# Retention: the next values are summed ahead of a unit's second rotation, and one of two barriers between the blocks is left out

## The reference, cut to what matters

```python
def rotary(t, pos):
    t1, t2 = t[..., :half], t[..., half:]
    return jnp.concatenate([t1 * cos - t2 * sin, t2 * cos + t1 * sin], -1)

def retention(q, k, v):                     # q and k rotated, blocks of 128 tokens
    scores = jnp.einsum('bnihd,bnjhd->bnhij', qc, kc) * dmask[None, None]
    inner = jnp.einsum('bnhij,bnjhe->bnihe', scores, vc)
    kv = jnp.einsum('bnjhd,hj,bnjhe->bnhde', kc, zeta, vc)
    def step(state, kv_n):
        return g_chunk[None, :, None, None] * state + kv_n, state
    _, prev = lax.scan(step, zeros, jnp.moveaxis(kv, 1, 0))
    cross = jnp.einsum('bnihd,hi,bnhde->bnihe', qc, xi, prev)
    return (inner + cross).reshape(b, lp, h, dv)
```

## Time and profile before

| what | us |
|---|---|
| median of 3 runs | 2862.14 (2860.37 to 2864.8) |
| the profiled execution | 2878.77 |
| its span, first to last instruction | 2876.9 |
| TensorE busy in the span | 2799.6 (97%) |
| VectorE busy | 1707.1 (59%) |
| GpSimd busy | 1347.0 (47%) |
| ScalarE busy | 621.4 (22%) |
| retention, first to last product (line 1053) | 151.9 to 624.1 |
| the granted TensorE clock, mean | 0.994 of full |

### The profile page before, as it was taken

How to read it: one execution, slowest core, us unless ns; L and a number is a source line. 1 busy time by engine, 2 the same in 40 slices (tenths; PEclk the granted TensorE clock), 3 DMA queues, 4 the chain that set the end, 5 groups by cost and what they waited for, 6 DMA issues and landing times.

```text
span 2876.9 us, 40988 instructions
## 1 busy us (share of the span) xinstructions
PE 2799.6 (97%) x14586; PEld 2066.1 (72%) x14586; DVE 1707.1 (59%) x4617; ACT 621.4 (22%) x1276; POOL 1347.0 (47%) x1140
## 2 busy tenths in 40 slices
PE   8999999999999999998999989999999999999997
PEld 4488888888876666664555767878878777787765
DVE  6655656657347777773777445677677772323226
ACT  2222222210025555551101101011111111111115
POOL 3533434547731111111455245677667665565535
PEclk9999999999999999999999999999999999999999
DMA  6500010111121113006444357899899989999986
GB/s 223 188 6 17 15 46 1 30 30 30 44 64 38 62 40 134 25 29 241 151 144 154 125 223 227 257 290 278 270 281 286 283 278 296 307 301 311 316 248 253
DMA packets 192573, 470.52 MB, mean 164 GB/s; under 512 B 27384, under 2 KB 108104, under 8 KB 166632
## 3 DMA queue, kind: packets, MB, share of 16 engines
q1 hardware_dynamic: 145424, 347.63, 33.8%
q0 software_dynamic: 44640, 111.84, 16.7%
q10 hardware_dynamic: 2304, 8.39, 0.7%
HBM read 349.64 MB, written 118.11 MB: 163 GB/s over the span
## 4 chain that ended last, share of the span: by engine, by line
PE 39%; DMA 7%; POOL 3%; DVE 3%; issue 2%; SPq 1%; ACT 0%; POOLq 0%; DVEq 0%; ACTq 0%
PE ps L3067 18%; PE ps L2842 7%; PE ps L3015 4%; DMA moe_xg<-t_rows,index 4%; PE ps L2986 3%; PE ps L2898 3%; DMA base_rows<-moe_yo,index 3%; PE ps L2983 2%; DVE moe_xT L2143 1%; POOL moe_xg L2569 1%; PE ps L2908 1%; POOL base_rows L2590 1%; PE ps L2861 1%; POOL moe_fin L2651 1%; PE ps L2852 0%
## 5 line engine op out<-in xcount | busy, mean ns | idle before, releaser
L2569 POOL DMA_INDIRECT moe_xg<-t_rows,index x433 | 426.7, 985 | 173.9 <-issue 133.8
L3067 PEld LDWEIGHTS ps<-moe_xT,moe_wg 128*128 128x128 f32 x2048 | 352.4, 196 | 56.6 <-issue 36.8
L3067 PE MATMUL ps<-moe_xT,moe_wg 128*128 128x192 f32 (+22 forms) x2048 | 379.6, 338 | 11.3 <-DVE moe_hh L2043 8.3
L3067 PE MATMUL ps<-moe_xT,moe_wu 128*128 128x192 f32 (+22 forms) x2048 | 376.7, 337 | 0.0
L2590 POOL DMA_INDIRECT base_rows<-moe_yo,index x100 | 229.2, 2292 | 278.3 <-DVE moe_yo L2157 99.0
L2143 DVE STREAM_TRANSPOSE moe_xT<-moe_xg 128x256 f32<-128x256 f32 x433 | 235.2, 609 | 207.6 <-DMA moe_xg<-t_rows,index 190.8
L3067 PEld LDWEIGHTS ps<-moe_xT,moe_wu 128*128 128x128 f32 x2048 | 354.4, 197 | 4.9
L2706 ACT ACTIVATE moe_sl<-ps 128x256 f32<-128x256 f32 (+19 forms) x144 | 49.6, 345 | 946.6 <-PE ps L3067 763.9
L1342 POOL TENSOR_TENSOR fox_diag<-fox_c,fox_causal 128x128 f32<-128x128 f32 x128 | 55.7, 456 | 417.1 <-DVE fox_mx L1371 412.3
L1365 DVE CUSTOM_DVE_ANT_0 hT<-ps,fox_c 128x512 f32<-128x512 f32 (+7 forms) x320 | 166.5, 560 | 77.4 <-PE ps L1634 77.2
L2198 DVE SCALAR_TENSOR_TENSOR moe_yo<-ps,weight,moe_yo 128x512 f32<-128x512 f32 (+14 forms) x280 | 187.4, 740 | 26.9 <-ACT moe_yo L2729 20.9
(11 more groups left out here) (376 smaller groups left out, 5013.2 us busy)
## 6 DMA issues: line engine op xcount, KB each, us to landing
moe_wg<-in_we_gate SPq DMA_DIRECT2D x64, 1024.0 KB
moe_wu<-in_we_up SPq DMA_DIRECT2D x64, 1024.0 KB
moe_wd<-in_we_down SPq DMA_DIRECT2D x64, 1024.0 KB
fox_c<-ck SPq DMA_DIRECT2D x8, 1032.0 KB, 8.8
emb_xin<-in_x SPq DMA_DIRECT2D x16, 512.0 KB, 3.9
h_rows<-emb_hr SPq DMA_DIRECT2D x16, 512.0 KB, 2.8
ret_w<-in_w_in SPq DMA_DIRECT2D x16, 512.0 KB, 6.6
moe_yt<-h_rows SPq DMA_DIRECT2D x16, 512.0 KB
```

The source lines that it names most:

```text
L2569: pool.indirect_dma_start(out=xg[g % NXG][:, :], out_offset=None, in_=quarters, in_offset=bass.IndirectOffsetOnAxis(ap=route.index4[:, AT4 ...
L3067: ins = pe.matmul(out, w[:, c, f:FF:FC], xT[u][:, c, 0:n], start=(c == 0), stop=(c == DC - 1))
```

## The change

`values(U, 0)` moves on VectorE's queue from the head of the next unit to the place between `follow(U)` and `rotate_block(U, 1)`; the call behind the loop for the last unit goes. And `Phase.reset` no longer ends with a meeting of all engines.

```diff
         nc.clear_and_free_semaphores(cls.used)
         cls.used = []
-        nc.all_engine_barrier()
...
             for U, (h, j) in enumerate(STEPS):
                 if U >= 1:
                     ph_, n0, n1 = before(U)
-                    values(U - 1, 0)
                     if j == 1:
                         update(h, 0)
                     mask(ph_, n0)
...
                 follow(U)
+                values(U, 0)
                 rotate_block(U, 1)
                 if U >= 1:
                     stats(ph_, n1)
             ph_, n0, n1 = before(len(STEPS))
-            values(len(STEPS) - 1, 0)
             mask(ph_, n0)
```

## The result

| kernel | median us | runs |
|---|---|---|
| before | 2861.26 (2859.77 to 2864.80) | 4 |
| changed | 2982.72 (2977.66 to 2984.39) | 4 |

The ratio is 1.0408, with a 95% interval of 1.0395 to 1.042: 121.5 us more, where 79.6 were forecast and 2962 was the end of the range. Of the two profiled executions the changed one took 105.6 us more (2984.39 against 2878.77). Up to the barrier between the blocks it is 119.5 us late (the meeting is over at 1427.1 instead of 1307.6 us); the block of the experts then ran 13.8 us shorter in this pair of profiles, and a change of 119.5 us up to there fits the medians.

The account below looks back on a forecast made before the run. TensorE, busy for 97% of the span, was taken as the bound. Seam costs of 84.7 us, less 4.8 recovered and 0.3 for the barrier, gave +79.6 us: 2862.1 to 2941.7 us, with an 8-in-10 range of 2910 to 2962.

Parts of the forecast that it names:

- The moved sum, the seam: Retention seams: second rotation held by GpSimd's token sums, mask late for 1086; a plain seam costs 2.3 us.
- The kinds of seams: 30 retention seams: 16 plain at 2.3 us, 9 at 4.4, 2 at 3.4, 3 head changes at 0.1 in all.
- The sum of the waits: Retention stage: all seams and the last unit together 84.7 us, less 4.8 us taken back, 79.9 us.
- The clock: TensorE's clock behind the 11 seams with 3.4 and 4.4 us waits: 0 to 16 us possible, taken as 0.
- The rival: TensorE's clock falls in the long waits of the retention stage: +16 us on top, 2958 us; chance 0.11.
- The recovered waits: TensorE's three waits for ScalarE's scaled values in the retention stage vanish: 4.8 us taken back.
- The barrier: Meeting at line 138: leaving it out saves 0.3 us of GpSimd's way, bounds 0 to -0.5 us.
- More get through: Seams: two rotation instructions pass at each change of GpSimd's sums, seam costs 0.9 us; +20, 2882 us; chance 0.11.
- fewer get through: Seams: the rotation's 4th product misses the gap of 265 and 267; +20 us, 2962 us; chance 0.05.
- not slower: Same rotation: token sums do not hold it, cover of 1.7 us hides the mask; 2857 us, 0.18% less; chance 0.07.

Follow-up runs that it names:

- the filled kernel: Changed kernel plus 352 unread TensorE matmuls in front of 1084's group, or of 1073 behind a head's first unit: 1.0297 of before, 83.7 us more.
- the kernel filled in the long waits only: Changed kernel with unread extra matmuls only in the 15 seams where TensorE waits 3 us or more: 1.0299 of before, 87.8 us more.
- the run with the sums behind 267 held: Changed kernel, but what stands directly behind GpSimd's token sums waits for the seam's second rotation: 1.0282 of before, 81.2 us more.
- the move alone: Changed kernel with the barrier of line 138 put back: 1.0403 of before, 115.6 us more.

## Why the prediction was wrong

The direction and the mechanism were right, the size was not: +79.6 us forecast, +121.5 measured. By its steps:

- **The moved sum, the seam.** Right to a tenth of a us, the rotation's ends to a hundredth or two. They were forecast at P+1.42, 2.71, 3.97, 4.2, 5.45 and, in a plain seam, 5.67; in the seams at 374 and 394 us they were at P+1.43, 2.71, 3.98, 4.19, 5.46 and 5.66. The mask began at P+5.99 (forecast 6.08), 1084 at P+6.30 (6.41), with a sum behind 266 at P+8.44, with a short one at P+7.36. The plain seam at 394 us, whose P is 394.45:

```profile
399.83 0.28 DVE L889 TENSOR_TENSOR ret_r<-ret_cosd,ret_sind 128x128 f32<-128x128 f32 x1
...
400.44 0.26 DVE L952 TENSOR_TENSOR ret_sT<-ps,ret_rc 128x128 f32<-128x128 f32 x1
...
400.75 0.49 PE L1084 MATMUL ps<-ret_vg,ret_sT 128*128 128x128 f32 x2 [2.04 <-DVE ret_sT L952]
```

With the clock kept up, a plain seam took 16.6 us against 14.3, one with a weight sum 18.8: 2.3 and 4.5 us more, where 2.3 and 4.4 were forecast. The changes of heads had no wait, as forecast.

- **The kinds of seams.** One was mis-sized. Behind a head's first unit TensorE needs the state's first update (964 after) at line 1073, before it needs the mask, and this update stood behind the held rotation too. The prediction counted these four seams as plain ones; with the clock kept up they took 18.8 us (the first 18.4), where 14.9 is the old seam, so 3.5 to 3.9 each and not 2.3 to 2.6: about 5 us in all. The run with the update in front showed it. Such a seam (P is 314.91):

```profile
320.27 0.28 DVE L889 TENSOR_TENSOR ret_r<-ret_cosd,ret_sind 128x128 f32<-128x128 f32 x1
...
320.88 0.26 DVE L964 COPY ret_S<-ps 128x128 f32<-128x128 f32 x1
...
321.06 0.28 POOL L772 TENSOR_SCALAR ret_ve<-ret_mv 128x16 f32<-128x16 f32 x1 [0.86 <-DVE ret_mv L959]
...
321.20 0.79 PE L1073 MATMUL ps<-ret_vz,ret_r 128*128 128x128 f32 x2 [3.63 <-DVE ret_S L964]
```

These rows also show why the roots held nothing in three of these seams, neither the 0.3 us each of the sum nor the up to 5.7 us that stood beside it: GpSimd's 772 waits for VectorE's statistics, so it and 774 began only when the rotation was over. What these three seams have over the first (3.9 against 3.5 us) is those statistics, which stand in front of the state's update.

- **The sum of the waits.** With the clock kept up by extra matmuls, the 29 distances between GpSimd's 30 waits were 80.6 us longer than before (510.44 against 429.87), the recovered 4.8 us taken off. The forecast for these 29 is 76.0: 79.9 without the 3.4 of the thirtieth seam and the 0.5 of the last unit. So the waits alone were forecast 4.6 us too low, and that is the state's 5.
- **The clock.** This is the step that failed: "I take 0, because the rest of such a unit is dense and 2.0 us did nothing." Against the filled kernel, the clock fell with all 13 waits of 3.2 to 4.2 us in these 29 distances and with 5 of the 12 of 2.04 us; of the two of 3.1 us it fell with the second, which lies behind the last distance, and not with the first. A fall cost 1.6 to 1.7 us, and 2.3 to 3.0 in the three seams where it began earlier, in all 32.3 us over the 29 distances. The rival had the mechanism but not the size (11 x 1.5 = 16 us): it left out the four seams of the state, and the plain ones, whose 2.0 us it took from a single row as harmless. That row showed one case that went well of a kind that goes badly in about a third: 12 of 36, over the two profiles of this kernel and that of the kernel filled in the long waits only, and 8 of 23 in the run with the sums behind 267 held. What decides which of them it is, no run here shows.
- **The recovered waits.** Right: the entry of the scaled values is gone. The run with the weight sums out of the way shows that they came from these collisions.
- **The barrier.** Right, nothing measurable.
- **The rivals.** "More get through" and "fewer get through" fell with the timeline; "not slower" fell too: a run comes near it only where GpSimd is made to wait. The two mis-sized terms, 32 and 5 us, point the same way and, with the one fall behind the last distance, account within 2 us for the 37.7 us by which the stage is longer than forecast (117.6 against 79.9). The range reached only to a clock term of 16 us or so and ended at 2962.

The Trainium skill says on its page "SBUF — State Buffer", section "SBUF: two separate sides", that the shared pair of ports is held for a whole instruction; the turns of 1.2 to 1.4 us and the run with halved sums agree. On its page "TensorE: Matmul & The Clock Gate", section "What's actually happening", it says that activity is what releases the clock; the filled kernel, whose clock stayed at 1.00, agrees.

## What to carry to other kernels

Before an instruction with two inputs in SBUF is moved, look at what GpSimd runs at its new place: each is held to the end of GpSimd's running instruction, so its price is the length of those, not its own. A new wait of TensorE of 2 us or more in a dense stage is to be priced twice, once as the wait and once, in part of the cases (12 of 36 at 2.04 us), for the lower clock behind it; every wait of 3.2 us or more had it in both profiles of the changed kernel. And follow every consumer of what stands behind a delayed instruction, the ones of a loop's first turn too.

## What the hardware showed that was not expected

- The clock mostly fell late: full through 4.2 us of idle time, then at the lower level for the first work behind it (362 to 366 us above). A look at the clock of the wait itself showed nothing in most seams, and in three of 19 it did (0.78 and 0.50 at 634 to 638 us).
- Work that nobody needs made the kernel 32 us faster (filled against the move alone), because it kept the clock up.
- Cutting GpSimd's instructions of 1.27 us into halves of 0.73 to 0.77 us took 80 us off the loss of 115.6, although GpSimd then works longer; nothing else in the program changed but the counts of the semaphore that goes with them.
